# Feed-forward upper products: two rows of parts as one moving operand of 512 columns

## The reference

```python
h2 = rms_norm(x, g_ffn[l])
gt = causal_dwconv(h2 @ w_ffn_gate[l], ffn_conv_w[l])
x = x + (jax.nn.silu(gt) * (h2 @ w_ffn_up[l])) @ w_ffn_down[l]
```

## Time and profile before

| | |
|---|---|
| median of 3 runs | 1911.15 us (1908.98 to 1918.33) |
| the profiled execution | 1914.11 us |
| its span, first to last instruction | 1912.3 us |
| mean granted TensorE clock | 0.965 of full speed |
| PE busy | 1804.9 us |
| DVE, ACT, POOL busy | 1174.4, 944.4, 318.0 us |
| the four upper stages | 134.0, 134.0, 132.5 and 132.7 us |

### The profile page before, as it was taken

One profiled execution on the slowest core, in us unless ns is written; L12 is line 12 of the kernel. 1 busy time (PEld: TensorE's weight loads), 2 busy tenths in 40 slices (PEclk: granted clock), 3 DMA queues, 4 the chain that ended last, 5 costly groups with the idle time before them and its releaser, 6 DMA issues.

```text
span 1912.3 us, 31649 instructions
## 1 busy us (share of the span) xinstructions
PE 1804.9 (94%) x13416; PEld 1691.9 (88%) x13416; DVE 1174.4 (61%) x1864; ACT 944.4 (49%) x1298; POOL 318.0 (17%) x71
## 2 busy tenths in 40 slices
PE   7999999989999999999999978799999978899998
PEld 7989999989889999998998877669998977779986
DVE  6976666666459767666664657556454734555453
ACT  5445564534455465645444545454334654454332
POOL 2611100345427120004355000000000000000000
PEclk9899999999999999999999989689999999899999
DMA  7684445545546644454555463124556644234562
GB/s 232 168 229 133 155 147 186 175 155 179 218 138 181 194 146 147 154 194 154 177 177 198 138 178 111 67 67 133 176 184 226 180 141 129 89 111 155 177 219 79
DMA packets 249148, 305.75 MB, mean 160 GB/s; under 512 B 9778, under 2 KB 224142, under 8 KB 249007
## 3 DMA queue, kind: packets, MB, share of 16 engines
q1 hardware_dynamic: 235959, 289.66, 47.2%
q10 hardware_dynamic: 13048, 14.07, 3.6%
HBM read 299.51 MB, written 4.19 MB: 159 GB/s over the span
## 4 chain that ended last, share of the span: by engine, by line
PE 66%; DVE 13%; ACT 8%; DMA 7%; issue 3%; ACTq 1%; POOL 0%; DVEq 0%; SPq 0%; POOLq 0%
PE psum L461 20%; PE psum L462 19%; PE psum L463 19%; DVE wlo L437 6%; ACT whi L429 4%; DMA raw<-in_b_w_q 2%; DMA raw<-in_w_in 2%; DMA raw<-in_a_w_in 1%; DVE hT L615 1%; ACTq L2454 1%; DMA raw<-in_b_w_out 1%; DMA raw<-in_ffn_w_up 1%; ACT work L2030 1%; ACT hidden L901 1%; PE psum L2397 1%
## 5 line engine op out<-in xcount | busy, mean ns | idle before, releaser
L429 ACT ACTIVATE whi<-raw 128x2048 fp32r<-128x2048 f32 (+2 forms) x277 | 525.4, 1899 | 318.2 <-PE psum L463 164.5
L461 PE MATMUL psum<-hT,whi 128*128 128x256 f32 x2160 | 621.2, 288 | 16.9 <-DVE wlo L437 16.9
L437 DVE TENSOR_TENSOR wlo<-raw,whi 128x2048 fp32r<-128x2048 f32 x213 | 505.3, 2380 | 193.8 <-PE psum L463 151.0
L462 PE MATMUL psum<-hT,whi 128*128 128x256 f32 x2160 | 615.2, 285 | 0.0
L463 PE MATMUL psum<-hT,wlo 128*128 128x256 f32 x2160 | 614.8, 285 | 0.0
L437 POOL TENSOR_TENSOR wlo<-raw,whi 128x2048 fp32r<-128x2048 f32 x64 | 316.8, 4951 | 743.1 <-PE psum L463 535.7
L461 PEld LDWEIGHTS psum<-hT,whi 128*128 128x128 f32 x2160 | 418.3, 194 | 24.2 <-DVE wlo L437 21.7
L462 PEld LDWEIGHTS psum<-hT,whi 128*128 128x128 f32 x2160 | 418.5, 194 | 0.2
L463 PEld LDWEIGHTS psum<-hT,wlo 128*128 128x128 f32 x2160 | 418.2, 194 | 0.0
L461 PE MATMUL psum<-whi,hT 128*128 128x256 f32 (+2 forms) x448 | 145.2, 324 | 1.1 <-issue 1.1
L462 PE MATMUL psum<-wlo,hT 128*128 128x256 f32 (+2 forms) x448 | 144.3, 322 | 0.0
(11 more groups left out here) (353 smaller groups left out, 2856.0 us busy)
## 6 DMA issues: line engine op xcount, KB each, us to landing
raw<-in_w_in SPq DMA_DIRECT2D x78, 1024.0 KB, 5.9
raw<-in_ffn_w_up SPq DMA_DIRECT2D x44, 1024.0 KB, 5.2
raw<-in_w_ffn_gate SPq DMA_DIRECT2D x22, 1024.0 KB, 5.4
raw<-in_w_ffn_up SPq DMA_DIRECT2D x22, 1024.0 KB, 5.3
raw<-in_w_ffn_down SPq DMA_DIRECT2D x22, 1024.0 KB, 4.9
raw<-in_ffn_w_down SPq DMA_DIRECT2D x22, 1024.0 KB, 5.1
raw<-in_b_w_q SPq DMA_DIRECT2D x12, 1024.0 KB, 5.2
raw<-in_a_w_in SPq DMA_DIRECT2D x10, 1024.0 KB, 5.3
```

What stands on the lines that cost most here:

```text
L429: act.activation(part(whi, n, HIGH_SLOTS), part(raw, n, RAW_SLOTS), ACT.Copy).then_inc(high_made, 1)
L437: eng.tensor_tensor(part(wlo, n, LOW_SLOTS), part(raw, n, RAW_SLOTS), part(whi, n, HIGH_SLOTS).bitcast(F32), ALU.subtract).then_inc(stream ...
L461: nc.tensor.matmul(dst, left[0], right[0], start=first, stop=False)
L462: nc.tensor.matmul(dst, left[0], right[1], start=False, stop=False)
```

## The change

From unit 4 on a unit's two tiles have a bank each. One product of 512 columns takes the high part of the weights against `hT[0]` and `hT[1]` side by side (`hT_both`): the first half of the bank becomes high x high, the second half high x low. A second product of 256 columns adds low x high to the first half. ACT copies the second halves of the two banks to SBUF (`copy_small`), and DVE adds them to the first halves (in `gate`, and in `product`). Eight banks are in use instead of four, so PE's waits for banks are written anew (`await_banks`). The low parts of all feed-forward weights are DVE's, and it makes them two by two at the end of a pair's work. ACT's work is put in another order, the high parts are made earlier relative to it. With convolution the scaling or adding of the gate moves from ACT to DVE.

```diff
         for c in range(FT // 2):
-            u += [(a["w_ffn_gate"][l][:, c * S:(c + 1) * S], "P"), (a["w_ffn_up"][l][:, c * S:(c + 1) * S], "PV"[c > 0])]
-        u += row_units(a["w_ffn_down"][l], FT, "PV")
+            u += [(a["w_ffn_gate"][l][:, c * S:(c + 1) * S], "V"), (a["w_ffn_up"][l][:, c * S:(c + 1) * S], "V")]
+        u += row_units(a["w_ffn_down"][l], FT, "V")
...
-        hT = [over(f"hT{i}", at_h, i * KT * S, [KT, S]) for i in range(2)]
+        hT_both = over("hT", at_h, 0, [2, KT, S])
+        hT = [hT_both[:, i] for i in range(2)]
...
+            def first_bank(n):
+                if n < RAW:
+                    return up + n
+                if n < 2 * pairs - 2:
+                    return (turned, turned + 2, up, up + 2)[(n - RAW) % 4]
+                return up + 2 * (n % 2)
...
+            def await_banks(pe, n):
...
+                if n == 2 * pairs - 2:
+                    taken = gate_scaled if conv is not None else inner_ready
+                    pe.wait_ge(taken.sem, taken.at(pairs - 1))
+                elif n >= RAW + 2:
+                    last = {6: 1, 7: 3, 2 * pairs - 1: 2 * pairs - 3}[n] if n in (6, 7, 2 * pairs - 1) else n - 4
+                    pe.wait_ge(bank_free.sem, bank_free.at(2 * (last // 2) + 2))
...
-                        mm = columns_product(pe, own(n), w, rows if n < RAW else hT)
+                        for j in range(2):
+                            b = bank(first_bank(n) + j)
+                            for k in range(KT):
+                                nc.tensor.matmul(b.rearrange("p (i s) -> p i s", i=2), w[0][:, k, j * P:(j + 1) * P],
+                                                 hT_both[:, :, k, :], start=k == 0, stop=False)
+                                mm = nc.tensor.matmul(b[:, 0:S], w[1][:, k, j * P:(j + 1) * P], hT[0][:, k, :],
+                                                      start=False, stop=k == KT - 1)
...
+                def copy_small(n):
+                    act.activation(small(n), small_tiles(n), ACT.Copy).then_inc(small_ready.sem, 1)
+
                 for c in range(pairs):
-                    make_high(act, n0 + 2 * c + 3)
                     act.wait_ge(bank_full.sem, bank_full.at(2 * c + 1))
...
                     if c >= 2:
-                        act.wait_ge(operand_ready.sem, operand_ready.at(c - 1))
-                    if 2 * c >= RAW:
-                        act.activation(gpad[:, c % 2, :, pad:], pair_of(2 * c), ACT.Copy).then_inc(scores_ready.sem, 1)
-                    make_high(act, n0 + 2 * c + 4)
+                        act.wait_ge(bank_free.sem, bank_free.at(2 * c - 2))
+                        copy_small(2 * c)
+                    make_high(act, n0 + 2 * c + 5)
                     silu(c)
-                    if c:
-                        high(c - 1)
-                high(pairs - 1)
-                make_high(act, n0 + 2 * pairs + HIGH_SLOTS)
+                    if c >= 2:
+                        act.wait_ge(bank_full.sem, bank_full.at(2 * c + 2))
+                        act.wait_ge(parts_ready.sem, parts_ready.at(c - 1))
+                        copy_small(2 * c + 1)
+                    make_high(act, n0 + 2 * c + 6)
+                    high(c)
...
                     if c >= 2:
                         dve.wait_ge(context_read.sem, context_read.at(c - 1))
-                    v_link(dve.tensor_tensor(prod[:, c % 2], cacc[:, c % 2], pair_of(2 * c + 1), ALU.mult))
+                    if 2 * c >= RAW:
+                        dve.wait_ge(small_ready.sem, small_ready.at(2 * c - RAW + 2))
+                        v_link(dve.tensor_tensor(u, u, small(2 * c + 1), ALU.add))
+                    v_link(dve.tensor_tensor(prod[:, c % 2], cacc[:, c % 2], u, ALU.mult))
...
                 for c in range(pairs):
-                    b = c % 2
+                    gate(c)
                     if c == 0:
-                        gate(0)
                         whole_rows(dve, turned)
-                    make_lows(dve, n0 + 2 * c + 2)
...
+                        short_conv(c)
+                    if c == 0:
+                        make_lows(dve, n0 + 4)
+                    else:
                         low(c - 1)
-                    make_lows(dve, n0 + 2 * c + 3 + (c == 0))
                     product(c)
                     if c == 0:
                         for b in range(4):
                             whole_low(dve, hT, turned, gain, b)
-                make_lows(dve, n0 + 2 * pairs + 2)
+                    make_lows(dve, n0 + 2 * c + 5)
                 low(pairs - 1)
```

More of the change, by code:

```diff
@@ L856, in ffn_up_stage, with tiles, small_tiles, small @@
             n0, rows = len(stream.freed), raw_T["ffn"]
[L857 to L863, removed]
+            RAW, up = 4, turned ^ 4
+            def first_bank(n):
[4 more added lines that the diff above has]
+                return up + 2 * (n % 2)
+            def tiles(n):
+                b = first_bank(n)
+                if n < RAW:
+                    return bank(b).rearrange("p (j s) -> p j s", j=2)
+                return psum[:, b:b + 2, 0:S]
+            def small_tiles(n):
+                b = first_bank(n)
+                return psum[:, b:b + 2, S:2 * S]
+            def small(n):
+                c = n // 2
+                if n % 2:
+                    return prod[:, c % 2]
+                return cacc[:, c % 2] if conv is None else gpad[:, c % 2, :, pad:]
+            def await_banks(pe, n):
+                if n == 3:
+                    pe.wait_ge(root_spread.sem, root_spread.at(1))
+                if n == RAW:
+                    whole_turned(pe)
+                if n == 2 * pairs - 2:
[4 more added lines that the diff above has]
+                    pe.wait_ge(bank_free.sem, bank_free.at(2 * (last // 2) + 2))
             @block.tensor
@@ L868, in _ @@
                     w = take_unit(pe, n0 + n)
[L869 to L874, removed]
+                    await_banks(pe, n)
                     if n == 0:
-                        mm = first_unit(pe, w, rows, [own(0)[:, j * S:(j + 1) * S] for j in range(2)], True)
-                    else:
-                        mm = columns_product(pe, own(n), w, rows if n < RAW else hT)
+                        mm = first_unit(pe, w, rows, [bank(up)[:, j * S:(j + 1) * S] for j in range(2)], True)
+                    elif n < RAW:
+                        mm = columns_product(pe, bank(first_bank(n)), w, rows)
+                    else:
+                        for j in range(2):
[5 more added lines that the diff above has]
+                                                      start=False, stop=k == KT - 1)
                     mm.then_inc(bank_full.sem, 1)
@@ L890, in silu @@
                     if conv is None:
-                        if 2 * c < RAW:
-                            act.wait_ge(gate_scaled.sem, gate_scaled.at(c + 1))
-                        ins = act.activation(cacc[:, c % 2], pair_of(2 * c), ACT.Silu)
+                        act.wait_ge(gate_scaled.sem, gate_scaled.at(c + 1))
+                        src = tiles(2 * c)
                     else:
                         act.wait_ge(operand_ready.sem, operand_ready.at(c + 1))
-                        ins = act.activation(cacc[:, c % 2], cacc[:, c % 2], ACT.Silu)
-                    ins.then_inc(inner_ready.sem, 1)
+                        src = cacc[:, c % 2]
+                    act.activation(cacc[:, c % 2], src, ACT.Silu).then_inc(inner_ready.sem, 1)
                 def high(c):
@@ L1003, in ffn_up_stage @@
             context_read.close(pairs)
+            gate_scaled.close(pairs)
+            small_ready.close(2 * pairs - RAW)
             hand_over(pairs)
             if conv is not None:
-                scores_ready.close(pairs - RAW // 2)
                 operand_ready.close(pairs)
-                side_free.close(1)
-            else:
-                gate_scaled.close(RAW // 2)
             close_turn()
```

66 lines of the change are left out of this document (29 added, 37 removed).

## The result

The changed kernel takes 1935.8 us (median of 4 runs, 1933.1 to 1938.9) where the kernel before takes 1910.1 on the same chip (4 runs, 1904.3 to 1918.3): a ratio of 1.0126, 95% interval 1.0094 to 1.0159. It is slower; the forecast was 1920, with 1898 to 1942 as its range.

A forecast was written before the change was run, and what follows sets the result against it. PE, 94% busy, bounded the kernel; the new order would make a loop through one load the bound. 2 x 3.4 with convolution plus 2 x 0.6 without gave 8 us, +9 with late loads: 1920 on 1911.15, range 1898 to 1942.

The forecast's parts named there:

- products: Upper stages, units 4 to 21: 5.58 us per unit instead of 5.76, 13 us in four stages if PE bounds.
- POOL: Convolution layers: 36 low parts go to DVE at 2.29 us each, the port lock goes, the stall before unit 5 shrinks.
- rival E: Upper stages: 512-column products in strips slow PE; at 0.34 us instead of 0.23, about +100 us; chance 0.07.
- the ring: Upper stages: loop from a low part's end through load, ACT and DVE to the next; 12.5 us, 12.3 without convolution.
- The order: Upper stages: the new order closes a loop through one load; PE waits about 1.2 us before every odd unit.
- C's time: Upper stages: rival in which the loop through the load doesn't bind and PE does; -34 us, 1877; chance 0.08.
- Rival D: Upper stages: paired loads share the engines, the first lands 1.1 us later per turn; +33, about 1950; chance 0.13.
- The sum: Four upper stages with following down units: +3.4 us per layer with convolution, +0.6 without, 8 together, +9 with late loads.
- (1): Upper stages: SP's load of unit 2c+6, from low part's end to high part's start; 5.5 us, 5.35 without convolution.
- one load in ten: Upper stages: if one load in ten of 30 turns is late, 1 to 2 us come on top.
- The down units' term: First two layers: PE waits 1.1 us per layer before the second down unit, for the low part of unit 23.
- A's own: Upper stages: range of the likeliest case, the loop closes as worked out; 1914 to 1927, 1920 in the middle; chance 0.60.

The follow-up runs named there:

- e2: Kernel after, with DVE making the low part of unit 2c+3 ahead of the product of pair c (from pair 1 on); 1874.5 us.
- e9: e2 with the 512-column product made as two of 256 columns; 1887.5 us.
- e4: e1 with the 512-column product made as two of 256 columns; 1887.3 us.
- e1: Kernel after, with ACT making the SiLU and the copy ahead of the high part of unit 2c+4 (from pair 2 on); 1878.1 us.
- e5: Kernel after, with 24 small unused products on PE behind unit 0 of the second upper stage, shifting the instruction fetches; 1913.7 us.
- e8: e2 with POOL making the low parts that it made before the change; 1873.1 us.
- e10: e2 with e5's 24 extra small products; 1871.1 us.

## Why the prediction was right, and where it was short

**What bounds the kernel, products, POOL.** Right. The products of 512 columns in strips keep 0.230 us in e2 (0.236 in the slower units), so rival E is out. *Products* (forecast: 0.18 per unit, 13 us in four stages if PE stays the bound) measured 13.0 in e9 against e2 and 9.1 in e4 against e1; in the kernel after the ring hides it. The stall before unit 5 went from 3.61 to 1.30 in stage 1 and from 4.26 to 1.73 in stage 2.

**The order.** Right in mechanism, and in stage 1 in size: 12.44 against 12.5, term by term above; unit 5 starts 2.7 us sooner, as forecast. That the ring is the cause is shown by e1 and e2, which open it at different places and both come to C's time. Rival D (the paired loads share the engines) is out: in stage 1 and in e5 the ring's load, the first of a pair, lands in 4.8 to 5.7; it is the second, outside the ring, that takes 5.2 to 7.7. The sign given for D, a period above 13, did come (13.1 and 13.2 on average in stages 3 and 4), and would have named the wrong cause: D makes every turn longer, and here only every second one was.

**The sum.** Short by 15.8 us in the median and by 14.2 in the table below, mainly in one term: (1), the load, with its "one load in ten", "1 to 2 us" late. Late are 12 of 32, by 0.6 to 2.5 us.

| us | forecast | e5, fetch moved | after |
|---|---|---|---|
| with convolution, both upper stages | +4.6 | +3.9 | +8.7 |
| without, both upper stages | +1.2 | -0.6 | +14.1 |
| wait before the second down unit, first two layers | +2.2 | +0.4 | +0.4 |
| late loads | +1 | none in the shifted stages | in the rows above |
| total | +9 | +3.7 | +23.2 |

With the fetches moved the upper stages are thus 3.3 us longer than before, not 5.8 (and 1.2 of the 3.3 are the 24 products' own), and the loads in step with the fetch cost 19.5 more, not 1. The down units' term was too large: of the two waits of 1.1 us one of 0.4 came (third layer, where none was forecast, had one of 0.7). The two errors have opposite signs, so 1920 was nearer than its parts, and that is luck. So is a part of the range: 1935.8 lies inside 1898 to 1942 but outside A's own 1914 to 1927, and the room above was put there for rival D, which didn't come. (The whole span of e5 is 3.2 us shorter than before's, although these stages are 3.3 longer. Of the 6.5 gained outside them 5.4 lie between the second and the third upper stage, where the longest stretch at half clock is 37.5 us before and 17.1 in e5.)

In stages 3 and 4 the late loads account for all of it: four of them, 1.4 to 2.5 over 5.1, are 7.2 and 7.8, and e5 differs from after by 7.2 and 7.5. In stage 2 the difference is 5.4. The four late loads land 3.8 us later in sum than the same loads in e5, and unit 21 starts 3.8 later; the other 1.6 is unit 21 itself, which PE runs partly at half clock (7.65 us to the first down product, 6.08 in e5).

The sign of it stood in the trace of before, and I used it wrongly: 11 of the 44 loads of the stages without convolution took 6.0 us or more there, one in four. The prediction took the load ended at 1379.89, 6.7 us, as a stray that one in ten would follow. The DMA view of before in its window (1373 to 1380), then in that of a timely load (1361 to 1368):

```profile
q8 instruction: 1, 0.02, 1.2%
raw<-in_ffn_w_up SPq DMA_DIRECT2D x2, 1024.0 KB, 6.5
```

```profile
q1 hardware_dynamic: 1777, 1.80, 79.7%
raw<-in_ffn_w_up SPq DMA_DIRECT2D x2, 1024.0 KB, 5.1
```

(6.5 is the median of two loads, 6.70 and 6.27.) The late load had a fetch beside it, the timely one had none. A median over 44 loads hides two kinds; what mattered was which kind the ring would meet, and how often.

## What to carry to other kernels

When an edit moves work behind a load, write down the whole loop from one buffer's release to the next and compare its length with the bound engine's work: here every engine had room, and one line at either of two places was worth 3%. When a wait in such a loop has two lengths in the trace, look for what runs beside the long one, and whether the edit changes how often it comes; a count of instructions per unit can do that. A wider product pays only where PE is the bound; the best version here, e2's order with the change's products, is about 2% faster than the kernel before (1871 to 1874 us in e2, e8 and e10), 13 us of that from the width and the rest from the order (e9 against the kernel before, 23).

## What the runs showed of the hardware

A fetch of 16 KB of instructions for PE that starts while a load of 1 MB is under way goes with a late landing of that load: in the ring of the kernel after 6.0 to 7.7 us instead of 5.0 to 5.5, far more than 16 KB are worth beside 1 MB. The twelve traces together say how close the tie is. Of 440 upper-stage weight loads that were issued with no other under way (or one with at most 0.3 us left), and with no fetch starting from 1.5 us ahead of the issue to 6 us behind it, none took over 5.8 us. Of 66 with a fetch starting 0.6 to 3.5 us behind the issue, 60 took 5.9 to 7.7. With a fetch starting 4.2 to 5 us behind it, 4 of 72 did. That the fetch is the cause is shown by e5, which moves it and nothing else of weight; how it delays the load (which engine or ring it holds up) no view here shows. In stage 1 no ring load was late.

Behind seven of the twelve late loads of the kernel after, where PE had stood for 1.8 to 3.0 us, the granted clock was at half, 1.2 GHz, for 3.4 us. Behind the other five, where PE had stood for 1.3 to 2.2 us, it stayed at full. In the upper stages of the kernel before this is seen only after the stalls of 3.61 and 4.26 us in the first two. PE of the kernel after, behind a wait of 2.58 us, and the window of the same stretch (0.68 is the mean clock):

```profile
1364.98 0.50 PE L909 MATMUL psum<-hT,whi 128*128 128x512 f32 x1 [2.58 <-DVE wlo L439]
1365.32 0.28 PE L911 MATMUL psum<-hT,wlo 128*128 128x256 f32 x1
...
1367.22 0.63 PE L909 MATMUL psum<-hT,whi 128*128 128x512 f32 x1
1367.64 0.41 PE L911 MATMUL psum<-hT,wlo 128*128 128x256 f32 x1
1367.86 0.63 PE L909 MATMUL psum<-hT,whi 128*128 128x512 f32 x1
```

```profile
1364.90:1370.20 5.30, 5.22 (x21) 4.51 (x22) 3.53 (x4) 0.06 (x1) 0.00 (x0) 0.68 0.81 256
```

At half clock the products start 0.42 and 0.22 us apart, at full clock 0.23 and 0.12, so the unit takes 7.2 us and not 5.6, and the copy behind it at 1377.95 waits for PE. In stages 3 and 4 that adds nothing that shows: the turns of the ring are longer by 7.1 and 7.5 us in sum, all but 0.1 of the stages' difference to e5, and the later landings sum to that. In stage 2 it is the 1.6 us of unit 21, which has no turn of the ring behind it.
